# Order of the y steps beside masks and decays in the SSD part of a two-layer hybrid decoder trunk

## What is computed

```python
seg = a_cum[:, :, :, None] - a_cum[:, :, None, :]
decay = jnp.exp(jnp.where(causal, seg, -jnp.inf))
cb = jnp.einsum("bclgn,bcsgn->bclsg", Cc, Bc)
y_diag = jnp.einsum("bclsgr,bcsgrp->bclgrp", cb[..., None] * decay, X)
...
y = ssd_chunked(xh, dt, a, bm, cm) + d_skip[:, None] * xh
y = y.reshape(bsz, s, SSM_D_INNER) * jax.nn.silu(z)
yg = y.reshape(bsz, s, SSM_GROUPS, SSM_D_INNER // SSM_GROUPS)
yg = yg * lax.rsqrt(jnp.mean(yg * yg, axis=-1, keepdims=True) + EPS)
y_ssm = (yg.reshape(bsz, s, SSM_D_INNER) * norm_g) @ w_ssm_out
```

## Time and profile before

| | |
|---|---|
| median of 3 runs | 2317.44 us (2317.39 to 2318.23) |
| profiled execution | 2317.45 us |
| its span, first to last instruction | 2315.4 us |
| mean granted TensorE clock | 0.995 |
| busy: TensorE, VectorE, ScalarE, GpSimd | 98%, 59%, 44%, 48% |

### The profile page before, as it was taken

The page is one execution under the profiler, slowest core; times in us unless marked ns, Lnnn a source line. Parts: engine busy times, 40 slices in busy tenths (PEclk is TensorE's granted clock), DMA queues, the critical chain, the costliest instruction groups (busy, mean ns, idle before and its releaser), DMA issues.

```text
span 2315.4 us, 32138 instructions
## 1 busy us (share of the span) xinstructions
PE 2274.4 (98%) x11808; PEld 1903.4 (82%) x11808; DVE 1372.5 (59%) x2079; ACT 1030.0 (44%) x1882; POOL 1105.3 (48%) x825
## 2 busy tenths in 40 slices
PE   7999999999999999999989999999999999999997
PEld 6888998888878888888878889988888788888886
DVE  7678767556653787877757777612566436422224
ACT  2566653266653342222335666533566434332331
POOL 1466555433444454444435555554334444644542
PEclk9999999999999999999999999999999999999998
DMA  6333336422224345545422433222222232332231
GB/s 253 116 96 117 107 105 191 155 74 73 74 74 164 109 141 209 184 180 193 152 98 89 125 109 101 88 96 91 74 73 74 73 118 91 109 100 93 99 100 46
DMA packets 94124, 267.18 MB, mean 115 GB/s; under 512 B 8528, under 2 KB 35536, under 8 KB 88592
## 3 DMA queue, kind: packets, MB, share of 16 engines
q1 hardware_dynamic: 73776, 237.73, 30.2%
q10 hardware_dynamic: 20192, 27.40, 3.9%
HBM read 260.77 MB, written 4.33 MB: 114 GB/s over the span
## 4 chain that ended last, share of the span: by engine, by line
PE 60%; issue 18%; POOL 8%; POOLq 8%; DVE 2%; DVEq 1%; PEld 1%; DMA 1%; ACTq 1%; ACT 0%; SPq 0%; PEldq 0%
PE gemm L552 13%; PE gemm L554 13%; PE gemm L553 13%; POOL w_lo L1900 8%; POOLq L1902 8%; PE gemm L575 3%; PE gemm L576 3%; PE gemm L577 3%; PE aux L617 3%; PE aux L796 2%; PE aux L726 2%; PE aux L834 2%; PE aux L740 1%; PE aux L735 1%; DMA ada_pe<-stream 1%
## 5 line engine op out<-in xcount | busy, mean ns | idle before, releaser
L1900 POOL TENSOR_TENSOR w_lo<-raw,w_hi 128x512 fp32r<-128x512 f32 x704 | 973.4, 1404 | 1068.8 <-ACT w_hi L949 1060.4
L949 ACT ACTIVATE w_hi<-raw 128x1024 fp32r<-128x1024 f32 x352 | 370.8, 1058 | 677.4 <-PE gemm L554 607.2
L552 PE MATMUL gemm<-h_hi,w_hi 128*128 128x512 f32 x1472 | 589.8, 401 | 0.8 <-issue 0.8
L554 PE MATMUL gemm<-h_hi,w_lo 128*128 128x512 f32 x1472 | 575.3, 391 | 0.0
L553 PE MATMUL gemm<-h_lo,w_hi 128*128 128x512 f32 x1472 | 574.1, 390 | 0.0
L554 PEld LDWEIGHTS gemm<-h_hi,w_lo 128*128 128x128 f32 x1472 | 276.7, 188 | 59.9
L552 PEld LDWEIGHTS gemm<-h_hi,w_hi 128*128 128x128 f32 x1472 | 277.4, 188 | 58.1 <-issue 4.6
L553 PEld LDWEIGHTS gemm<-h_lo,w_hi 128*128 128x128 f32 x1472 | 277.4, 188 | 56.1 <-issue 1.9
L552 PE MATMUL gemm<-op_hi,w_hi 128*128 128x512 f32 x608 | 238.6, 392 | 0.2
L554 PE MATMUL gemm<-op_hi,w_lo 128*128 128x512 f32 x608 | 236.8, 389 | 0.0
L553 PE MATMUL gemm<-op_lo,w_hi 128*128 128x512 f32 x608 | 236.6, 389 | 0.0
(11 more groups left out here) (210 smaller groups left out, 3387.6 us busy)
## 6 DMA issues: line engine op xcount, KB each, us to landing
raw<-stream SPq DMA_DIRECT2D x336, 512.0 KB
ada_late<-stream SPq DMA_DIRECT2D x30, 1024.0 KB, 4.9
seg<-decay_rows ACTq DMA_DIRECT2D x64, 256.0 KB, 3.3
ada_early<-stream ACTq DMA_DIRECT2D x40, 256.0 KB, 4.2
raw<-stream SPq DMA_DIRECT2D x32, 256.0 KB
ada_first<-stream SPq DMA_DIRECT2D x5, 1024.0 KB, 20.6
x<-xT SPq DMA_DIRECT2D x2, 2048.0 KB, 10.3
ada_pe<-stream SPq DMA_DIRECT2D x3, 1024.0 KB, 14.2
```

Of the source, the lines that this page charges most:

```text
L552: mm(o, w_hi[:, slot, k, cols], hi[:, k, :], start=k == 0, stop=False)
L554: last = mm(o, w_lo[:, slot, k, cols], hi[:, k, :], start=False, stop=k == KB - 1)
L949: A(w_hi[:, slot, ks], raw[:, slot, ks], ACT.Copy).then_inc(hi_ready, 1)
L1900: gp.tensor_tensor(w_lo[:, slot, ks], raw[:, slot, ks], w_hi[:, slot, ks].bitcast(F32), ALU.subtract)
```

## The change

On VectorE the low part of the block before and the next normed block go ahead of the wait and the mask. On ScalarE the high part (take_y) goes ahead of the decay and the fetch. Nothing is added or taken away.

```diff
@@ ScalarE @@
+                    for _, key in EXTRA.get(tick - 1, ()):
+                        if key[0] == "y":
+                            take_y(*key[1:])
                     if 0 <= tick + 1 < T_POST:
                         decay(tick + 1)
                     if 0 <= tick + 2 < T_POST:
...
                     for _, key in EXTRA.get(tick - 1, ()):
                         if l and key == ("x", 7, 0):
                             act.wait_ge(x_saved, 16)
-                        if key[0] != "cb":
+                        if key[0] not in ("cb", "y"):
                             takes[key[0]](*key[1:])
@@ VectorE @@
-                    if tick == 2:
-                        wait_freed(l, ("cd",))
-                    if 0 <= tick + 1 < T_POST:
-                        masked(tick + 1)
                     for _, key in EXTRA.get(tick - 1, ()):
                         if key[0] == "y":
                             y_low(*key[1:])
                     for _, key in EXTRA.get(tick, ()):
                         if key[0] == "y":
                             y_normed(*key[1:])
+                    if tick == 2:
+                        wait_freed(l, ("cd",))
+                    if 0 <= tick + 1 < T_POST:
+                        masked(tick + 1)
```

## The result

Timed in turns on one chip, 21 times each: the changed kernel 2320.78 us (2319.26 to 2321.86), the kernel before 2317.69 us (2317.06 to 2319.04), ratio 1.0013, 95% interval 1.0007 to 1.0019. It is slower by 3.1 us, where a gain of 1.2 us was forecast. The profiled execution took 2321.07 us with a span of 2319.2 us, 3.8 us longer than the span before.

A forecast was written before the change was run, and what follows sets the result against it. VectorE's unbroken chain was taken to set TensorE's second wait. Mask 31 leaving it saves 0.61 us per layer, ScalarE's and GpSimd's terms count 0: 2317.45 - 1.22 = 2316.2 us, range 2314.8 to 2318.8 us.

The forecast's parts named there:

- Where the diff reaches (four ticks a layer): Only group 0's y steps, ticks 27 to 30, meet a mask; the other twelve y steps of a layer keep their order.
- the second wait: TensorE's transposes of yn at tick 30, 0.64 us late per layer, set by VectorE's chain; 0.61 us was to go.
- the first: TensorE's transposes of yn at tick 28, 0.56 us late (layer 1: 0.53); expected to go whole but bring nothing alone.
- mask 31 is worth 0.61 us a layer: Mask 31 leaves VectorE's chain ahead of yn 30, so the tick-30 transposes start 0.61 us earlier in each layer.
- GpSimd's halves move by 1.0 and 1.3 us: GpSimd's low halves at ticks 28 and 29 start later because ScalarE's conversions do, moving onto other instructions of VectorE.
- The lateness of the decays, the tanh of z and the converted halves: ScalarE's later work in ticks 28 and 29 was put at cost 0, bounds 0 and 0.6 us per layer.
- I take 0 for the difference, since the same two halves meet the same kind and number of instructions: VectorE's losses beside GpSimd's moved halves, ticks 28 to 30: no net change, bounds -0.6 and +1.8 us per layer.
- the bound of +1.8: Upper bound per layer, in us, on VectorE's added loss beside GpSimd's halves: two collisions more.
- the second rival: GpSimd's shifted halves hit masks 29 and 30 and gate_y, 0.92 us each; two or more collisions per layer had chance 0.12.
- Its signs of being wrong: Masks of 1.6 us, idle before zt, waits for w_lo or a mask, second stall vanished; or over 3 us difference.
- The rival of two collisions: Two more GpSimd hits on VectorE per layer, +1.23 us each layer, 2319.9 us; two or more had chance 0.12.
- The range: 2314.8 to 2318.8 us, taking in the whole stall and a little more than one collision per layer.

The follow-up runs named there:

- the fastest two versions: Kernel before with y_normed of blocks 1 to 3 of group 0 at the head of VectorE's tick: 2314.09 us; the same with ScalarE's new order: 2313.88 us.

## Why the prediction was wrong

**Right.** Where the diff reaches (four ticks a layer); that TensorE waits for yn alone; that VectorE's chain, without idle time, sets the second wait, so that the first, although it goes, gives nothing; that mask 31 is worth 0.61 us a layer (taken out alone it brought the transposes to their place); that GpSimd's halves move by 1.0 and 1.3 us: they did, 288.08 against 287.01 (287.95 less the 0.94 us by which this trace is ahead) and 293.15 against 291.88. The lateness of the decays, the tanh of z and the converted halves was hidden, as said.

**The step that failed** is "I take 0 for the difference, since the same two halves meet the same kind and number of instructions". The number of instructions hit is indeed four in both orders, but what each loses is not the same: in the old order three of the four lost little (0.19, 0.30, 0.42 us) and one lost 1.09; in the new one three lost 1.07 each and one 0.32. Of the old order's 2.00 us the prediction had read only the 0.19 of yn 28. The term is +1.5 us a layer, inside the bound of +1.8 that stood beside it. The halves moved by one step and the masks by one step in the same direction, so that they met; I had worked out both moves and mask 29's hit, and then let them cancel. Doing the same for mask 30 (about 294.3, half from 294.1) and for zt behind it would have given three full hits, and the second rival, at 0.12, as the likeliest. Its signs of being wrong came: masks of 1.76 us, and a difference over 3 us.

**What was missing** is the clock. The rival of two collisions gave 2319.9 us for the waits alone; these measured 2.0 us more, 2319.7 us by the median of before. The rest, 1.1 us of the median, is a little less than one more stretch of half clock costs (1.49 us in the trace), and 18 of 21 runs have the clock for it; that it lies behind the wait in most of them, and not at the start of layer 1, is not shown. The prediction priced a wait of TensorE at its own length, and named no wait long enough to cost more. The range ended at 2318.8 us. It did not even hold the prediction's own bound of +1.8 us a layer, which gives 2319.8 us, nor the waits alone.

The page of the Trainium skill, "SBUF — State Buffer", section "SBUF: two separate sides", says that whichever of the two starts first holds the shared port pair for its whole instruction, and the other is blocked. The traces agree: the losses follow the time that GpSimd's instruction has left, with masks of 1.76 us inside a half, 0.68 with the half moved away, and y_low, which reads one input from PSUM, at 0.74 to 0.75 us in all of them. The rule spoke against this change, and I gave its mechanism too small a chance.

**Open.** Where the changed kernel's runs have their half clock, behind the wait in layer 0 or 1 or at the start of layer 1, was not taken apart; the one trace shows layer 0 and a longer stretch at the start of layer 1. Why the clock falls behind one wait of 2.0 us and not behind another stays open too. Why the fastest two versions gain 3.6 and 3.8 us where the waits of group 0 are 2.4 us was not settled either. Part of it is at the two layer ends: the eight small matmuls of line 625 took 1.05 us there in the first of them and 1.71 and 1.86 us in the kernel before; at the start of layer 1 PEclk is 0.88 (1180 to 1183 us) against 0.67 (1181 to 1184). But no run changed that place by itself.

## What to carry to other kernels

When an engine runs without a gap and another waits for it, put what is waited for at the head of its queue, not one place further up: here the move past the masks gave nothing or less wherever GpSimd ran beside them, and the move past all that yn did not need gave 3.6 us. When a reordering shifts the work of VectorE and GpSimd together, write down for each instruction with both inputs in SBUF how long GpSimd's instruction will still run when it starts: here the same number of hits cost 2.0 us in one order and 3.5 us in the other. And a wait of TensorE can cost more than its length: behind two of four waits of 2.0 us the clock fell and another 1.5 us were lost, behind waits for yn of up to 1.5 us never.

## What I had not expected of the hardware

The clock's share: 3.4 us at half clock after a wait of 2.0 us, about 1.5 us on top of the wait, after one such wait and not after another in the same execution. And ScalarE's order alone, with the same work and no new resource, cost 8 us: two masks in a layer that wait 0.3 and 1.7 us for their decays, and the half clock behind that. In the changed kernel, with VectorE's new order beside it, no mask waits, but the same ScalarE order still makes the difference between 2317.7 and 2320.8 us.
